# Gathering expert rows as quarter rows and turning them on the vector engine, in a one-layer hybrid encoder with a mixture of experts

## The reference

```
g_sel = argmax(t @ w_group)                        # one of 4 groups
top_v, top_i = top_k(expert logits of that group, 2)
gates = p_group * softmax(top_v)
experts = g_sel * 8 + top_i                        # two of 32 experts
...
xs = t_pad[row_tok].reshape(n_blocks, 128, 1024)   # rows sorted by expert, padded to blocks of 128
def run(xb, e):
    return (silu(xb @ wg[e]) * (xb @ wu[e])) @ wd[e]   # 1024 -> 512 -> 1024, float32
ys = map(run, xs, blk_exp) * row_gate
out = segment_sum(ys, row_tok)
```

## Time and profile before

| quantity | value |
|---|---|
| median of 3 runs | 3060.33 us (3057.9 to 3062.94) |
| the profiled execution | 3064.2 us, span 3062.5 us |
| granted PE clock, mean of the span | 0.956 of 2.4 GHz |
| PE busy | 2769.7 us, 90% of the span |
| DVE / ACT / POOL busy | 49% / 33% / 14% |
| experts: gate, up and down products | 321.6 + 316.3 + 323.8 us |
| experts: transposes of the rows (L1877) | 48.6 us in 368 instructions |
| DMA, mean over the span | 125 GB/s |

### The profile page before, as it was taken

One profiled execution on the slowest core, in us unless ns is written; L12 is line 12 of the kernel. 1 busy time (PEld: TensorE's weight loads), 2 busy tenths in 40 slices (PEclk: granted clock), 3 DMA queues, 4 the chain that ended last, 5 costly groups with the idle time before them and its releaser, 6 DMA issues. The chain is left out here.

```text
span 3062.5 us, 39432 instructions
## 1 busy us (share of the span) xinstructions
PE 2769.7 (90%) x12609; PEld 1704.0 (56%) x12610; DVE 1511.3 (49%) x2948; ACT 1022.0 (33%) x2269; POOL 427.5 (14%) x684
## 2 busy tenths in 40 slices
PE   8999999999999857889959999599999999999960
PEld 6677767776777634555655555344444444444430
DVE  2556555655565658888823554422323232323227
ACT  2333333333333236777725554001010101010108
POOL 2111111111111102222210011101101010101000
PEclk9999999999999969999979999699999999999985
DMA  6000000010000150000052221587755557575558
GB/s 235 32 32 24 34 31 31 24 37 31 27 24 31 45 204 15 11 8 8 8 163 85 90 93 55 189 306 265 287 205 219 205 219 288 219 288 215 216 198 303
DMA packets 167182, 382.82 MB, mean 125 GB/s; under 512 B 12850, under 2 KB 30002, under 8 KB 164928
## 3 DMA queue, kind: packets, MB, share of 16 engines
q1 hardware_dynamic: 152800, 333.75, 30.1%
q0 software_dynamic: 14304, 48.08, 4.2%
HBM read 310.73 MB, written 71.08 MB: 125 GB/s over the span
## 5 line engine op out<-in xcount | busy, mean ns | idle before, releaser
L657 PE MATMUL z_psum<-w_in_sb,hT 128*128 128x512 f32 x1088 | 480.5, 592 | 0.0
L651 PE MATMUL z_psum<-hT,w_in_sb 128*128 128x128 f32 x3264 | 375.2, 276 | 0.8 <-ACT hT L327 0.8
L651 PEld LDWEIGHTS z_psum<-hT,w_in_sb 128*128 128x128 f32 x3264 | 371.0, 193 | 1.7 <-ACT hT L327 1.2
L1896 PE MATMUL gate_psum<-w_gate_sb,block_rows_T 128*128 x720 | 321.6, 600 | 12.6 <-SPq L1728 11.6
L1920 PE MATMUL down_psum<-w_down_sb,hidden_T 128*128 x720 | 323.8, 593 | 0.9 <-ACT hidden_T L1802 0.9
L657 PEld LDWEIGHTS z_psum<-w_in_sb,hT 128*128 128x128 f32 x1088 | 200.6, 190 | 220.9 <-issue 220.9
L1900 PE MATMUL up_psum<-w_up_sb,block_rows_T 128*128 x720 | 316.3, 592 | 0.0
L1605 PE MATMUL y_psum<-w_out_sb,mix_T 128*128 128x512 f32 x544 | 244.3, 603 | 0.9 <-DVE mix_T L1462 0.9
L847 ACT ACTIVATE probs_map<-score_psum,neg_max 128x512 f32<-128x512 f32 (+3 forms) x320 | 196.7, 624 | 110.4 <-DVE neg_max L897 110.3
L1900 PEld LDWEIGHTS up_psum<-w_up_sb,block_rows_T 128*128 128x128 f32 x720 | 136.9, 190 | 172.1 <-issue 172.1
L1896 PEld LDWEIGHTS gate_psum<-w_gate_sb,block_rows_T 128*128 128x128 f32 x720 | 135.1, 193 | 167.3 <-issue 167.3
(11 more groups left out here) (309 smaller groups left out, 3529.7 us busy)
## 6 DMA issues: line engine op xcount, KB each, us to landing
w_gate_sb<-in_w_e_gate SPq DMA_DIRECT2D x32, 2048.0 KB, 8.4
w_up_sb<-in_w_e_up SPq DMA_DIRECT2D x32, 2048.0 KB, 14.3
w_down_sb<-in_w_e_down SPq DMA_DIRECT2D x32, 2048.0 KB, 18.1
expert_rows<-scratch_moe SPq DMA_DIRECT2D x17, 1024.0 KB, 8.3
w_in_sb<-in_w_in SPq DMA_DIRECT2D x7, 2048.0 KB, 18.6
scratch_z<-z_ring SPq DMA_DIRECT2D x34, 256.0 KB, 2.0
scratch_h<-h SPq DMA_DIRECT2D x17, 512.0 KB, 2.6
x_tile<-in_x_prompt SPq DMA_DIRECT2D x16, 512.0 KB, 3.6
```

Of the source, the lines that this page charges most:

```text
L651: mm = pe.matmul(out[:, hd * P:(hd + 1) * P], w[:, c, col:col + P], hT[:, u, c, :], start=(c == 0), stop=(c == DC - 1))
L657: mm = pe.matmul(out[:, :], hT[:, u, c, :], w[:, c, g * HW:(g + 1) * HW], start=(c == 0), stop=(c == DC - 1))
L1896: mm = pe.matmul(gps[:, :], xT[:, u, c, :], part(wg, slot, c), start=(c == 0), stop=(c == DC - 1))
```

## The change

The rows of a block are no longer gathered as whole rows. A token's row of 1024 floats is seen as four quarter rows of 256 floats, and lane i (0 to 3) of the block is the group of its rows 32i to 32i+31. One indirect DMA per lane puts quarter j of the row 32i+r onto partition 32j+r. A 32x32 transpose on DVE then gives the layout that the products want, straight from SBUF to SBUF: partition 32j+s holds the columns 256j+32c+s for all 128 rows. PE's eight transposes, the PSUM tile and the two copies from PSUM are gone. Since the 128 columns of chunk c are others than before, the gate and up weights are permuted in DRAM to match, before the kernel starts; their transfers keep their shapes.

`mix_and_route` builds `row_all` (4 quarter-row numbers for every partition and block: four times the token plus the lane of the partition) in place of `tok_all`, which takes a wider copy, four more transposes and wider conversions at its end.

```
+            for j in range(LANES):
+                nc.vector.memset(lane[j * SQ:(j + 1) * SQ, :], float(j))
...
-            cp(blk[:, :], blk_rows[:, :]).then_inc(blk_ok, 1)
+            cp(blk[:, :], blk_rows[:, :])
+            cp(blk4[:, :, :, :], <blk_rows, each lane's 32 rows repeated 4 times>).then_inc(blk_ok, 1)
             dve.wait_ge(blk_ps, 1)
-            chain.after(cp(slot_all[:, :], yps[:, 0, 0:P]))
-            ts(tok_all[:, :], slot_all[:, :], 0.5, -0.25, ALU.mult, ALU.add)
+            chain.after(ts(tok4[:, :], yps[:, 1, :], 0.5, -0.25, ALU.mult, ALU.add))
+            cp(slot_all[:, :], yps[:, 0, 0:P])
+            ts(row_all[...], tok4[...], float(LANES), lane[:, 0:1], ALU.mult, ALU.add)
...
+            for i in range(LANES):
+                mm = pe.transpose(yps[:, 1, i * P:(i + 1) * P], blk4[:, i, :, :]..., ident[:, :])
+            mm.then_inc(blk_ps, 1)
...
             def gather(b, u):
-                wait(pool, x_ps, b - 1)
-                pool.tensor_copy(toks[:, u:u + 1], col(tok_all, b)).then_inc(tok_ok, 1)
+                wait(pool, xT_ok, b - 1)
+                pool.tensor_copy(toks[:, u, :], row_all[:, bass.ds(b, 1), :]...).then_inc(tok_ok, 1)
                 pool.wait_ge(tok_ok, b + 1)
-                pool.indirect_dma_start(out=xg[:, u, :], out_offset=None, in_=dr["h2"],
-                                        in_offset=bass.IndirectOffsetOnAxis(ap=toks[:, u:u + 1], axis=0)).then_inc(x_in[u], 16)
+                for i in range(LANES):
+                    pool.indirect_dma_start(out=xg[:, u, i, :], out_offset=None, in_=dr["h2"].rearrange("t (j d) -> (t j) d", j=LANES),
+                                            in_offset=bass.IndirectOffsetOnAxis(ap=toks[:, u, i:i + 1], axis=0)).then_inc(x_in[u], 16)
...
             gather(2, 0)
+            gather(3, 1)
             scatter(0, 0)
-            gather(3, 1)
+            gather(4, 0)
             scatter(1, 1)
             with pool.Fori(1, n) as i:
-                gather(i * 2 + 2, 0)
+                gather(i * 2 + 3, 1)
                 scatter(i * 2, 0)
-                gather(i * 2 + 3, 1)
+                gather(i * 2 + 4, 0)
                 scatter(i * 2 + 1, 1)
...
-            def copy_x(b, u):                                    # on DVE, and its other half on ACT
-                dve.wait_ge(x_ps, b + 1)
-                cp(xT[:, u, 4:8, :]..., xps[:, 1, :]).then_inc(x_dve, 1)
+            def turn_x(b, u):                                    # on DVE
+                dve.wait_ge(x_in[u], ...)
+                wait(dve, u_ps, b)
+                nc.vector.transpose(xT[:, u, :, :].rearrange("p c (i r) -> p c i r", r=SQ),
+                                    xg[:, u, :, :].rearrange("p i (c s) -> p c i s", s=SQ)).then_inc(xT_ok, 1)
...
-            copy_x(0, 0)
+            turn_x(0, 0)
+            turn_x(1, 1)
             hidden(0)
-            copy_x(1, 1)
...
             def gate_up(b, u):
-                pe.wait_ge(x_act, b + 1)
-                pe.wait_ge(x_dve, b + 1)
+                pe.wait_ge(xT_ok, b + 1)
...
-                down(b - 1, 1 - u, lambda: turn_x(b + 1, 1 - u))
+                down(b - 1, 1 - u)
```

More of the change, by code:

```diff
@@ L19 @@
 QUEUE = TILES * P
+SQ = 32
+LANES = P // SQ
 PAD_ROWS = P // 2
@@ L1203, in mix_and_route @@
     y, gates, trips, last_run = keep["y"], keep["gates"], keep["trips"], keep["last_run"]
-    slot_all, tok_all = keep["slot_all"], keep["tok_all"]
+    slot_all, row_all = keep["slot_all"], keep["row_all"]
     with ExitStack() as ctx:
@@ L1257, in mix_and_route @@
         blk = sb("block_queue_floats", [P, P])
+        blk4 = sb("block_queue_by_lane", [P, LANES, LANES, SQ])
+        tok4 = sb("token_by_lane", [P, LANES * P], U32)
+        lane = sb("lane_number", [P, 1])
         mps = ps("mix_T_psum", [P, 2, HW])
@@ L1582, in _ @@
             dve.wait_ge(blk_in, 16)
-            cp(blk[:, :], blk_rows[:, :]).then_inc(blk_ok, 1)
+            cp(blk[:, :], blk_rows[:, :])
+            cp(blk4[:, :, :, :], blk_rows[:, :].rearrange("p (i r) -> p i r", r=SQ)[:, :, None, :].to_broadcast([P, LANES, LANES, SQ])).then_inc(blk_ok, 1)
             dve.wait_ge(blk_ps, 1)
-            chain.after(cp(slot_all[:, :], yps[:, 0, 0:P]))
-            ts(tok_all[:, :], slot_all[:, :], 0.5, -0.25, ALU.mult, ALU.add)
+            chain.after(ts(tok4[:, :], yps[:, 1, :], 0.5, -0.25, ALU.mult, ALU.add))
+            cp(slot_all[:, :], yps[:, 0, 0:P])
+            ts(row_all[:, :, :].rearrange("p b i -> p i b"), tok4[:, :].rearrange("p (i b) -> p i b", i=LANES), float(LANES), lane[:, 0:1],
+               ALU.mult, ALU.add)
         @block.tensor
@@ L1653, in _ @@
             pe.wait_ge(blk_ok, 1)
-            pe.transpose(yps[:, 0, 0:P], blk[:, :], ident[:, :]).then_inc(blk_ps, 1)
+            pe.transpose(yps[:, 0, 0:P], blk[:, :], ident[:, :])
+            for i in range(LANES):
+                mm = pe.transpose(yps[:, 1, i * P:(i + 1) * P], blk4[:, i, :, :].rearrange("p j r -> p (j r)"), ident[:, :])
+            mm.then_inc(blk_ps, 1)
 def experts(nc, dr, consts, keep):
     ident = consts["ident"]
-    trips, slot_all, tok_all = keep["trips"], keep["slot_all"], keep["tok_all"]
+    trips, slot_all, row_all = keep["trips"], keep["slot_all"], keep["row_all"]
     FC = D_EXP // P
@@ L1671, in experts @@
         slots = sb("block_slots", [P, 2], U32)
-        toks = sb("block_tokens", [P, 2], U32)
-        xg = sb("block_rows", [P, 2, D])
+        toks = sb("block_tokens", [P, 2, LANES], U32)
+        xg = sb("block_rows", [P, 2, LANES, D // LANES])
         xT = sb("block_rows_T", [P, 2, DC, P])
@@ L1773, in _ @@
             gather(2, 0)
+            gather(3, 1)
             scatter(0, 0)
-            gather(3, 1)
+            gather(4, 0)
             scatter(1, 1)
             with pool.Fori(1, n) as i:
-                gather(i * 2 + 2, 0)
+                gather(i * 2 + 3, 1)
                 scatter(i * 2, 0)
-                gather(i * 2 + 3, 1)
+                gather(i * 2 + 4, 0)
                 scatter(i * 2 + 1, 1)
             scatter(n * 2, 0)
-            pool.wait_ge(x_in[1], n * 16 + 16)
+            pool.wait_ge(x_in[0], n * 64 + 128)
+            pool.wait_ge(x_in[1], n * 64 + 64)
             pool.wait_ge(o_out, n * 32 + 16)
@@ L1788, in _ @@
             n = load(act, trips[0:1, 0:1], 1, MAXT)
-            def copy_x(b, u):
-                act.wait_ge(x_ps, b + 1)
-                nc.scalar.copy(xT[:, u, 0:4, :].rearrange("p c t -> p (c t)"), xps[:, 0, :]).then_inc(x_act, 1)
             def gate(b):
@@ L1830, in _ @@
             n = load(dve, trips[0:1, 0:1], 1, MAXT)
-            def copy_x(b, u):
-                dve.wait_ge(x_ps, b + 1)
-                cp(xT[:, u, 4:8, :].rearrange("p c t -> p (c t)"), xps[:, 1, :]).then_inc(x_dve, 1)
+            def turn_x(b, u):
+                half = b // 2 if isinstance(b, int) else None
+                dve.wait_ge(x_in[u], 64 * half + 64 if half is not None else (b - u) * 32 + 64)
+                wait(dve, u_ps, b)
+                nc.vector.transpose(xT[:, u, :, :].rearrange("p c (i r) -> p c i r", r=SQ),
+                                    xg[:, u, :, :].rearrange("p i (c s) -> p c i s", s=SQ)).then_inc(xT_ok, 1)
             def hidden(b):
@@ L1852, in blk @@
                 hidden(b)
-                copy_x(b + 1, 1 - u)
+                turn_x(b + 1, 1 - u)
                 copy_out(b - 1, 1 - u)
-            copy_x(0, 0)
+            turn_x(0, 0)
+            turn_x(1, 1)
             hidden(0)
-            copy_x(1, 1)
             blk(1, 1)
@@ L1869, in _ @@
             n = load(pe, trips[0:1, 0:1], 1, MAXT)
[L1871 to L1878, removed]
             def run_of(b):
@@ L1908, in turn_a, with down @@
                 mm.then_inc(a_ps, 1)
-            def down(b, u, middle=None):
+            def down(b, u):
                 run, slot = run_of(b)
@@ L1916, in down @@
                 for half in range(2):
-                    if half and middle:
-                        middle()
                     for c in range(FC):
@@ L1932, in _ @@
             pe.sem_inc(d_ps, 1)
-            turn_x(0, 0)
             gate_up(0, 0)
-            turn_x(1, 1)
             turn_a(0, 0)
@@ L2073 @@
         a = _np.ascontiguousarray(inputs[name])
+        if name in ("w_e_gate", "w_e_up"):
+            a = _np.ascontiguousarray(a.reshape(1, N_EXP, LANES, DC, SQ, D_EXP).transpose(0, 1, 3, 2, 4, 5).reshape(a.shape))
         if a.ndim == 1:
```

7 lines of the change are left out of this document (3 added, 4 removed).

## The result

The changed kernel takes 3035.69 us (median of 4 runs, 3034.39 to 3042.63) where the kernel before took 3061.64 in the same comparison: a ratio of 0.9921, 95% interval 0.9902 to 0.994, or some 24 us less by the ratio (26 by the two medians). 3037 was predicted. The profiled execution after took 3034.39 us with a span of 3032.7. That is 29.8 less than the profiled execution of before, but 5.7 us of it lie ahead of anything that the change touches (the number table of the queue is converted at 1937.86 and not at 1943.52), and that is no part of the gain.

The account below looks back on a forecast made before the run. PE's stream was taken to bound the middle of the experts stage, with DMAs close behind in places. -35.7 + 8.0 + 2.5 + 2.3 = -22.9 us took the median of 3060.3 to 3037.4, forecast 3037, own range 3031 to 3043.

Parts of the forecast that it names:

- the chains of single blocks: Three places in the experts stage with three runs of one block in a row, where DMAs were to set the pace.
- PE's transposes, 41 sets: Experts stage behind the fifth block's gate: 41 sets of 0.87 us leave PE's stream, -35.7 us.
- three chain waits: Gates behind three single-block runs: PE waits 2.7 us for weights each time, +8.0 us in all.
- start, first gather to fifth gate: Start of the experts stage, at the DMAs' pace: dearer gathers and one more before the first scatter, +2.5 us.
- end of routing: Ahead of the barrier before the experts stage: wider conversions and four more transposes, +2.3 us (1.7 to 3).
- DVE's transpose: Each block, between `hidden` and the output copy: 1.3 us where 6.4 are free, hidden behind the down products.
- the margin of 2.55: Single-block chain in the kernel before: SP's word for the weights came 2.55 us before PE's gate needed it.
- The price of a quarter row: Gather of each block: 1 KB pieces at 50 ns cost 0.4 us more per gather on all 16 engines.
- The first rival: Experts stage: quarter rows make the DMAs the bound at 1.7 us more per gather, +10 us, 3071; chance 0.08.
- The fourth rival: Behind the chain waits: PE's clock drops, each of the three costing 3.2 us more, 3047; chance 0.15.

Follow-up runs that it names:

- the second trace: The changed kernel run once more without further edits, as the measure for the other runs: 3041.59 us, ratio 0.9926 to the kernel before.
- with whole rows: The changed kernel with the gather (one DMA of 128 whole rows) and end of routing of before, DVE's transposes kept: 3038.67 us, ratio 0.9922 to the kernel before.
- PE's time put back: The changed kernel with eight idle transposes per block in PE's old place, into spare PSUM: 3061.72 us, ratio 1.0 to the kernel before.
- SP's numbers ahead: The changed kernel with SP loading the numbers for its next fetches before its waits for the landings: 3020.52 us, ratio 0.986 to the kernel before.
- The gathers of half rows: The kernel before with three more gathers of 128 half rows (2 KB pieces) per block, into a spare tile: 3089.34 us.

## Why the prediction was right, step by step

The mechanism came out as predicted: PE's stream gets shorter by its transposes, and the chains of single blocks give part of it back because there the fetches set the pace. That the sum came so close is luck: the lower clock, which it put at nothing, cost 6.7 us, and the drain, which it did not have, brought 6.5. Term by term, from the two profiled executions:

| step | predicted us | measured us |
|---|---|---|
| PE's transposes, 41 sets | -35.7 | -35.9 (41 times 21.915 less 21.04) |
| three chain waits | +8.0 | +8.9 (2.88 + 3.08 + 2.91) |
| low clock behind them | 0 | +3.6 (two gates of 8.82) |
| start, first gather to fifth gate | +2.5 | -0.3; +0.5 to +2.7 in six other runs with quarter rows |
| the fifth gate's own clock | 0 | +3.1 (10.19 against 7.13 us; 8.83 in the second trace) |
| end of routing | +2.3 | +2.2 |
| POOL's drain | not seen | -6.5 |
| sum | -22.9 | -24.9 |

The two executions differ by 24.1 us once the 5.7 us ahead of the change are taken off; 0.8 us stay unassigned.

*PE and DVE.* The period was predicted to 0.01 us. DVE's transpose took 1.234 us on the mean of 46, where 1.3 was taken from the nearest row, and hides with 5.2 us to spare. The Trainium skill, "Vector Engine (DVE) Microarchitecture Reference", section 3.8, led to an estimate of 1.1 us; the trace shows 12% more.

*The chains.* They stand where the earlier trace rows put them, and each wait is 2.9 to 3.1 us against 2.7. PE's gain of 3.5, less the margin of 2.55, plus 1.93 by which the links became longer, gives 2.9. The prediction gave the links 1.7 more, 1.4 of it for dearer pieces. The runs divide it otherwise: with whole rows the three links still last 1.2 us more than before in the first chain (75.27) and 1.8 more in the second (75.88 against 74.07), and quarter rows add 0.7 and 0.1 to that. With PE's time put back they last 75.05 and 74.65, 1.0 and 0.6 more than before. So the pieces bring 0.1 to 1.0, less than the 1.4. And the prediction says that the DMAs set the pace here; that is only part of it. In the first link their share is 0.98 from 2092 to 2110 us but 0.79 over the whole link, and with SP's numbers ahead the three links get 2.4, 2.8 and 3.1 us shorter: SP's pause between a landing and the next fetch is on the path too.

*The price of a quarter row* is the mis-sized term: 0.4 us per gather was taken, some 0.07 measured. I had read it off transfers with rows of 512 B and 2 KB, which are cut into packets of those sizes. Here four pieces share one packet of 4 KB, by the packet counts, and so the 50 ns per 1 KB piece that the prediction looked for don't exist. The gathers of half rows agree: one block's DMAs take 528 packets there, which is two pieces to a packet; one packet to a piece would be 720. The Trainium skill, "DMA: Bandwidth & Descriptors", section "Why small descriptors are slow (HBM only)", speaks of joining consecutive descriptors into packets; whether that is what happened here no run shows. The Trainium skill's rule in that section had led to an estimate of 0.1 us, nearer than the rows. The first rival needed 1.1 us per gather and was far off.

*The clock.* The fourth rival was half right, and I should have put part of it into the sum: two of the three gates in one execution and all three in the other ran for a part at the lower level, 1.8 us each and not 3.2. The length of the wait doesn't tell which: 3.08 us left the clock at 1.00, and 2.23 us with whole rows did not.

*The end of the stage* is the step that I did not have. Between the last scatter and the next stage the kernel before loses 11.86 us; I did not read that stretch, since nothing in it is edited. Without its 6.5 us the sum would be -18, and 3042 the time: inside the range, but five above the forecast.

## What to carry to other kernels

When work leaves the engine that bounds, look for the next pace-setter where its margin is smallest, and ask what that one waits for. Here it was some 3 us of number loading between a landing and the next fetch, free to remove: worth 15 to 21 us after the change, and before it 3 us that are not clear of noise. And read the gaps at the ends of a stage too, drains and barriers included, even where the change edits nothing there.

## What the runs showed of the hardware

- A 32x32 transpose of 128x1024 float32, SBUF to SBUF, takes 1.234 us on DVE; four in a row 5.07, six 7.63.
- Indirect gathers of 1 KB pieces went out as packets of 4 KB, four pieces to one. With the 16 completions for each further DMA they cost some 0.07 us more per block of 128 rows on 16 engines than whole rows (0.045 by another trace).
- POOL's drain at the end of a stage took from 1.05 to 9.05 us, repeatable to some ns for one list of indirect DMAs and unmoved by 64 further instructions; its rule is open.
- Waits of PE of 2.2 to 3.1 us leave the clock at 1.00 in some cases and at 0.81 over the next 8.8 us in others, in the same kernel.
